# First two layers of a six-layer transformer pass: the norm at each seam by token tile instead of by column half

## The reference, cut to what matters

```
h = rms_norm(x, pre_mix_norm[l])
proj = h @ w_in[l]                       # 1024 x 2464
mix = concat(four attentions(proj))      # 256 x 1024
mix = mix @ w_o[l]
x = x + rms_norm(mix, post_mix_norm[l])
h = rms_norm(x, pre_ffn_norm[l])
gate, up = split(h @ ffn_w_gate_up[l])   # 1024 x 5632
f = (silu(gate) * up) @ ffn_w_down[l]    # 2816 x 1024
x = x + rms_norm(f, post_ffn_norm[l])
# rms_norm(x, w) = x * rsqrt(mean(x*x) + 1e-6) * w
```

## Time and profile before

| | |
|---|---|
| median of 3 runs | 1873.91 us (1871.16 to 1876.33) |
| profiled execution | 1872.82 us, span 1871.0 us |
| TensorE busy | 1823.4 us, 97% of the span |
| VectorE, ScalarE, GpSimd busy | 65%, 51%, 6% |
| mean granted TensorE clock | 0.996 of full speed |
| weights read | 309.90 MB, 167 GB/s over the span |

### The profile page before, as it was taken

How to read it: one execution, slowest core, us unless ns; L and a number is a source line. 1 busy time by engine, 2 the same in 40 slices (tenths; PEclk the granted TensorE clock), 3 DMA queues, 4 the chain that set the end, 5 groups by cost and what they waited for, 6 DMA issues and landing times.

```text
span 1871.0 us, 26055 instructions
## 1 busy us (share of the span) xinstructions
PE 1823.4 (97%) x9972; PEld 1533.6 (82%) x9972; DVE 1207.3 (65%) x1741; ACT 952.7 (51%) x1322; POOL 110.7 (6%) x152
## 2 busy tenths in 40 slices
PE   7999999999999999999999999999999999999999
PEld 6778888877888878788888788888778888878887
DVE  6576656867666588765565566557766556766555
ACT  5574444566544467644445554445254445665443
POOL 1400000150000030000000000003300001000000
PEclk9999999999999999999999999999999999999999
DMA  7604565641555656155554335554725554525552
GB/s 257 193 23 168 182 201 190 185 166 41 172 183 184 219 165 209 35 181 199 183 211 150 135 133 188 203 195 159 206 91 198 201 185 166 194 91 179 190 203 79
DMA packets 186216, 313.00 MB, mean 167 GB/s; under 512 B 17886, under 2 KB 69396, under 8 KB 186132
## 3 DMA queue, kind: packets, MB, share of 16 engines
q1 hardware_dynamic: 182883, 304.24, 48.3%
q0 software_dynamic: 1104, 3.50, 0.8%
q10 hardware_dynamic: 2144, 4.12, 0.7%
HBM read 309.90 MB, written 1.94 MB: 167 GB/s over the span
## 4 chain that ended last, share of the span: by engine, by line
PE 57%; DVE 4%; ACT 1%; issue 0%; POOL 0%; ACTq 0%; DVEq 0%
PE acc L2143 10%; PE acc L2144 10%; PE acc L2145 10%; PE up L2713 5%; PE tr L2713 5%; PE tr L2720 3%; PE up L2720 3%; PE acc L2713 2%; DVE tiles L1988 1%; PE acc L2720 1%; PE acc L2461 1%; PE up L2143 1%; PE up L2145 1%; PE up L2144 1%; PE tr L2321 1%; PE up L2422 1%
## 5 line engine op out<-in xcount | busy, mean ns | idle before, releaser
L1515 DVE TENSOR_TENSOR w_lo<-raw,w_hi 128x2048 fp32r<-128x2048 f32 (+2 forms) x290 | 654.5, 2288 | 177.1 <-ACT w_hi L1014 175.6
L1014 ACT ACTIVATE w_hi<-raw 128x2048 fp32r<-128x2048 f32 (+2 forms) x290 | 534.0, 1879 | 104.2 <-PE tr L2720 55.9
L2143 PE MATMUL acc<-w_hi,hT 128*128 128x512 f32 (+3 forms) x672 | 260.9, 388 | 3.2 <-DVE w_lo L1515 1.2
L2145 PE MATMUL acc<-w_hi,hT 128*128 128x512 f32 (+3 forms) x672 | 257.7, 383 | 0.0
L2144 PE MATMUL acc<-w_lo,hT 128*128 128x512 f32 (+3 forms) x672 | 257.4, 383 | 0.0
L2143 PE MATMUL acc<-w_hi,aux_hi 128*128 128x512 f32 x608 | 237.1, 390 | 0.0
L2144 PE MATMUL acc<-w_lo,aux_hi 128*128 128x512 f32 x608 | 237.1, 390 | 0.0
L2145 PE MATMUL acc<-w_hi,aux_lo 128*128 128x512 f32 x608 | 236.5, 389 | 0.0
L2713 PE MATMUL up<-hT,w_hi 128*128 128x512 f32 x768 | 191.6, 391 | 0.7 <-DVE w_lo L1515 0.7
L2713 PE MATMUL tr<-hT,w_hi 128*128 128x512 f32 x768 | 189.7, 389 | 0.0
L2713 PEld LDWEIGHTS tr<-hT,w_hi 128*128 128x128 f32 x768 | 144.2, 188 | 29.9
(11 more groups left out here) (386 smaller groups left out, 2249.6 us busy)
## 6 DMA issues: line engine op xcount, KB each, us to landing
raw<-in_mlp_w_up SPq DMA_DIRECT2D x64, 1024.0 KB, 6.5
raw<-in_mlp_w_down SPq DMA_DIRECT2D x64, 1024.0 KB, 5.4
raw<-in_ffn_w_gate_up SPq DMA_DIRECT2D x88, 512.0 KB, 4.7
raw<-in_ffn_w_down SPq DMA_DIRECT2D x22, 1024.0 KB, 5.0
raw<-in_w_in SPq DMA_DIRECT2D x16, 1024.0 KB, 8.7
raw<-in_sb_w_in SPq DMA_DIRECT2D x12, 1024.0 KB, 5.3
raw<-in_moba_w_in SPq DMA_DIRECT2D x12, 1024.0 KB, 5.4
raw<-in_w_o SPq DMA_DIRECT2D x8, 1024.0 KB, 6.2
```

Source lines behind the costliest of these rows:

```text
L1014: nc.scalar.activation(w_hi[:, p0.slot, 0:p0.floats], raw[:, p0.slot, 0:p0.floats], ACT.Copy)\
L1515: nc.vector.tensor_tensor(w_lo[:, p0.slot, 0:m], raw[:, p0.slot, 0:m], f32(w_hi[:, p0.slot, 0:m]), ALU.subtract).then_inc(sem["lo_ready"], 1)
L2143: nc.tensor.matmul(dst, hi, whi, start=first, stop=False)
L2145: return nc.tensor.matmul(dst, lo, whi, start=False, stop=last)
```

## The change

At the four seams everything goes by token tile.

- `closing` (w_o's last column half): token tile outside, pieces inside. `tile_done` follows tile 0's eight k, `piece_used` each piece's use by tile 1. Before the last two k of tile 1 TensorE transposes the first 512 columns of tile 0's new x (`turn_of`). The feed-forward's last step raises `tile_done` for each of its blocks.
- VectorE makes the root by tile (`y_root`), adds 512 columns of one tile at a time, and puts hT_lo of tile 0 between (`turned_lo_of`, 128 wide).
- The filler matmuls go; four transposes at a time (`turn_of`) stand between parts of the next matrix.
- `opening` (w_in and its like) does tile 0's high products, then its low ones, then tile 1. `first_hidden` (feed-forward, step 0) does three of the four hidden tiles for 128 tokens first, then for the other 128; the fourth hidden tile stays 256 wide.
- The plan: behind a feed-forward of these layers the turn of slots goes on with slot 3 (`align(3)`), so the next matrix's first piece has a slot that the feed-forward doesn't use; its split stands ahead of the last hidden step's sums on ScalarE and VectorE.

The core of the diff:

```diff
@@ class Plan
-    def align(self):
-        self.ring_start = len(self.pieces)
+    def align(self, slot=0):
+        self.ring_start = len(self.pieces) - slot
@@ make_plan, behind a feed-forward of layers 0 and 1
-            plan.align()
+            plan.align(3)
...
@@ ScalarE: gemm
                     if ph.out == "y":
                         act.wait_ge(sem["tile_done"], n["tile_done"] + i + 1)
                         y_square(sum_bank(ph, i, 0), 0, i)
+                        if i == len(ph.chunks) - 1:
+                            turned_hi(ph.then, 0, 0)
                         act.wait_ge(sem["piece_used"], pieces[-1][0] + 1)
                         y_square(sum_bank(ph, i, 1), 1, i)
...
@@ VectorE: gemm, last column half of w_o
+                            y_root(t)
+                            if t == 0:
+                                y_added(0, 0, W)
+                                y_gain(ph, sum_bank(ph, i, 0), 0, i)
+                                y_added(0, W, D)
+                                turned_lo_of(ph.then, 0, 0)
+                            else:
+                                y_added(1, 0, W)
+                                turned_lo_of(ph.then, 0, 1)
+                                y_gain(ph, sum_bank(ph, i, 1), 1, i)
+                                y_added(1, W, D)
...
@@ VectorE: feed-forward, behind the last step
+                    gain(0, 0)
+                    dve.wait_ge(sem["y_sq"], n["y_sq"] + 2)
+                    y_root(0)
+                    y_added(0, 0, W)
+                    gain(0, 1)
+                    y_added(0, W, D)
+                    dve.wait_ge(sem["y_sq"], n["y_sq"] + 4)
+                    y_root(1)
+                    gain(1, 0)
+                    y_added(1, 0, W)
+                    turned_lo_of(ph.then, 0, 0)
+                    turned_lo_of(ph.then, 0, 1)
+                    gain(1, 1)
+                    y_added(1, W, D)
...
@@ TensorE
+            def turn_of(base, t, half):
+                pe.wait_ge(sem["x_written"], base + 2 * t + half + 1)
+                for k in range(PK * half, PK * half + PK):
+                    last = nc.tensor.transpose(turned_tile(t, k), x[:, t, P * k:P * k + P], ident)
+                last.then_inc(sem["hT_tr"], 1)
...
+            def opening(ph):
...
+                one, two = pieces
+                pe.wait_ge(sem["lo_ready"], one[0] + 1)
+                high(0, *one)
+                turn_of(base, 0, 1)
+                pe.wait_ge(sem["lo_ready"], two[0] + 1)
+                high(0, *two)
+                turn_of(base, 1, 0)
+                low(0, *one)
+                low(0, *two)
+                turn_of(base, 1, 1)
+                for piece in pieces:
+                    high(1, *piece)
+                    low(1, *piece).then_inc(sem["piece_used"], 1)
...
+            def closing(ph, i, n0, w, pieces):
+                for t in range(TT):
+                    for p, k0, kt in pieces:
+                        slot = plan.pieces[p].slot
+                        if t == 0:
+                            pe.wait_ge(sem["lo_ready"], p + 1)
+                        whi, wlo = piece_view(w_hi, slot, 0, kt, w), piece_view(w_lo, slot, 0, kt, w)
+                        for k in range(kt):
+                            kk = k0 + k
+                            if (t, k0, k) == (1, PK, 2):
+                                turn_of(n["x_written"], 0, 0)
+                            last = three(sum_bank(ph, i, t), hT_hi[:, kk, P * t:P * t + P], hT_lo[:, kk, P * t:P * t + P],
+                                         whi[:, k, :], wlo[:, k, :], kk == 0, kk == KT - 1)
+                        if t == 1:
+                            last.then_inc(sem["piece_used"], 1)
+                    if t == 0:
+                        last.then_inc(sem["tile_done"], 1)
...
+            def first_hidden(ph):
...
+                early = (0, 1, 2)
+                pe.wait_ge(sem["lo_ready"], ph.first + 1)
+                high(0, 0, P, early)
+                low(0, 0, P, early)
+                pe.wait_ge(sem["lo_ready"], ph.first + 2)
+                high(1, 0, P, early)
+                turn_of(base, 1, 0)
+                low(1, 0, P, early)
+                high(0, P, S, early)
+                turn_of(base, 1, 1)
+                low(0, P, S, early)
+                high(0, 0, S, (3,))
+                low(0, 0, S, (3,)).then_inc(sem["piece_used"], 1)
+                high(1, P, S, early)
+                low(1, P, S, early)
+                high(1, 0, S, (3,))
+                low(1, 0, S, (3,)).then_inc(sem["piece_used"], 1)
```

More of the change, by code:

```diff
@@ L342, in make_plan @@
             a.then, b.before = b, ("y" if a.out == "y" or a.variant == "A" else "x")
+            if b.before == "y":
+                b.counts.update({"hT_tr": 2 * TT, "hT_hi": TT * KT, "hT_lo": TT * KT})
         if a.kind == "norm":
@@ L1427, in ffn @@
                     early = ph.variant == "B" and steps[0] == 0
+                    final = steps[0] == ph.n - 1
                     if early:
@@ L2226, in gemm @@
                             pe.wait_ge(sem["evac_d"], n["evac_d"] + i - 1)
+                    if ph.opens is not None and ph.opens.before == "y" and i == 0:
+                        opening(ph)
+                        continue
+                    if ph.out == "y" and i == len(ph.chunks) - 1:
+                        closing(ph, i, n0, w, pieces)
+                        continue
                     for p, k0, kt in pieces:
@@ L2656, in mix_conv, with weights @@
                 keep_clock(tr[:, 0, 0:S], 3)
[L2658 to L2660 removed]
+            def first_hidden(ph):
+                base, hi, lo = n["x_written"] - Y_WRITES, n["hT_hi"] - TT * KT, n["hT_lo"] - TT * KT
+                slots = [plan.pieces[ph.first + j].slot for j in range(ph.ups)]
+                def weights(buf, j, a, k):
                     at = PK * CH_A * (a // 2) + CH_A * k + P * (a % 2)
[L2662 to L2676 removed]
@@ new lines, in weights, with high @@
+                    return buf[:, slots[j], at:at + P]
+                def high(j, first, end, which):
+                    for k in range(PK):
+                        kk = PK * j + k
+                        pe.wait_ge(sem["hT_hi"], hi + KT * (end // P - 1) + kk + 1)
+                        for a in which:
+                            dst, src = first_sums[a][:, first:end], hT_hi[:, kk, first:end]
+                            nc.tensor.matmul(dst, weights(w_hi, j, a, k), src, start=kk == 0, stop=False)
+                            nc.tensor.matmul(dst, weights(w_lo, j, a, k), src, start=False, stop=False)
@@ new lines, in low @@
+                def low(j, first, end, which):
+                    for k in range(PK):
+                        kk = PK * j + k
+                        pe.wait_ge(sem["hT_lo"], lo + KT * (end // P - 1) + kk + 1)
+                        for a in which:
+                            last = nc.tensor.matmul(first_sums[a][:, first:end], weights(w_hi, j, a, k), hT_lo[:, kk, first:end],
+                                                    start=False, stop=kk == KT - 1)
+                    return last
@@ L2681, in hidden @@
                 def hidden(i, steps):
-                    for j in range(ph.ups):
+                    if ph.variant == "A" and steps[0] == 0:
+                        first_hidden(ph)
+                    for j in range(ph.ups if ph.variant == "B" or steps[0] > 0 else 0):
                         ps_ = [plan.pieces[ph.first + j if c == 0 else ph.first + ph.ups + ph.per * (c - 1) + j]
```

165 lines of the change are left out of this document (78 added, 87 removed).

## The result

| | before | after |
|---|---|---|
| median | 1874.82 us (4 runs, 1871.16 to 1876.33) | 1885.60 us (4 runs, 1883.98 to 1886.55) |
| ratio | | 1.0058, 95% interval 1.0046 to 1.0071 |
| profiled execution, span | 1872.82 us, 1871.0 us | 1885.99 us, 1884.1 us |

The changed kernel is 0.6% slower. Of its profile, first the page's busy times (the counterpart of the earlier trace rows): TensorE has 96 matmuls more (144 by the halved products, 48 fewer by the filler) and stays at 97%.

What follows compares the result with a forecast made beforehand. TensorE, busy 97% of the span, was taken as the bound, with gains only from its gaps. 3.55 + 8.75 + 1.5 - 0.5 - 2.2 + 0.3 = +11.4 us, giving 1885 us; range 1871 to 1893.

Steps and rivals of the forecast that it cites:

- Price of the narrow matmul: Feed-forward opening: a matmul of 128 columns behind a 128-column load costs 0.1115 us, between 0.060 and 0.125.
- The 0.060 row: Profile row with 30 weight columns loaded, 128 columns going every 0.06 us; taken as the lower bound of the price.
- First seam: w_o to feed-forward in layer 0: waits hidden, 20.6 us against 17.07, +3.55 us.
- Third seam: w_o to feed-forward in layer 1: +3.55 and a 5.2 us TensorE wait behind a late-freed slot, +8.75 us.
- Rival 2: No stall in layer 1: the slot is free in time or the wait passed otherwise; +4.7, 1878 us, chance 0.09.
- rival 1: Cheap loads: an fp32r load of 128 weight columns hides under 128 streamed columns; -3.6, 1870 us, chance 0.14.
- Clock behind it: Behind layer 1's stall after w_o: the idle stretch may lower TensorE's clock; 1.5 us put in, between 0 and 3.4.
- Second seam: Feed-forward to next input matrix in layer 0: early end paid back as a wait for w_lo, -0.5 us.
- Fourth seam: Feed-forward to next input matrix in layer 1: one VectorE split now ahead of its gains, -2.2 us (0 to -2.8).
- Layer 2's output matrix: Left one slot off by the ring; its feed-forward's second piece split some 5 us later, +0.3 us.
- The sum: Whole kernel: the terms add to +11.4 us on 1872.8, carried over to 1885 us, 0.6% slower.
- Rival 3: Clock falls in the opening, narrow matmuls at 0.213 us; +18 to +30, 1895 us, chance 0.07.

Runs made afterwards that it cites:

- e2: Changed kernel with two hidden tiles instead of three made for the first 128 tokens alone; 1882.02 us, 1.0047 of the kernel before.
- e3: Changed kernel, early part of the first feed-forward step streaming only 64 of 128 tokens per tile behind the same weight loads; 1916.95 us, one run.
- e4: Changed kernel with the split of the feed-forward's second piece behind tile 0's square and turn; 1878.24 us, 1.0021 of the kernel before.
- e1: Changed kernel with the turn of slots begun anew with slot 0 before w_o; 1881.38 us, 1.0042 of the kernel before.
- e12: Changed kernel with 11 filler matmuls of 256 columns in layer 1 ahead of the transposes TensorE waits for; 1884.63 us, one run.
- e13: Kernel before with only the shifted turn of slots and the early split of the next matrix's first piece; 1873.12 us, 0.9991 of the kernel before.
- e10: Changed kernel with layer 1's feed-forward in slots 3, 0 and 1 instead of 0, 1 and 2; 1884.84 us, 1.0055 of the kernel before.
- e6: Changed kernel without the shifted turn of slots and the early split; 1881.68 us, 1.0037 of the kernel before.
- e8: Changed kernel with w_o and the first feed-forward step as in the kernel before; 1871.22 us, 0.9985 of the kernel before.
- e5: Changed kernel with 40 filler matmuls of 256 columns in layer 1 ahead of the transposes TensorE waits for; 1894.83 us, one run.

## Why the prediction was right

- **Price of the narrow matmul, 0.1115 us.** Measured 0.11, and 2.50 us a tile (e2). It came from the row with one streamed column, and e3 shows why that row was the right one: behind this load 1, 64 and 128 streamed columns cost the same. The 0.060 row had another load.
- **First seam, all waits hidden, +3.55.** Measured +3.63.
- **Third seam, the wait.** Place, chain and size held: 5.05 us for 5.2, and each link stands in the trace at the forecast distance. e4 takes it away by the place of the split, e1 by the slot. Rival 2 is refuted by the wait itself, rival 1 by the price.
- **Clock behind it, 1.5 taken between 0 and 3.4.** 1.76 by e12. That a clock loss comes was argued from the earlier trace rows, but 1.5 was picked and not worked out, so that it lies this near is luck; behind the same stall in e2 the loss was 0.3 less. The whole seam is 10.64 for 10.25: 3.63 + 5.05 + 1.76 = 10.44. Most of the missing 0.2 is how a wait is counted: the 5.05 begin at the end of a record of 0.39 us, and by starts, as everything else here, it is 478.40 - 472.96 - 0.23 = 5.21.
- **Second seam, -0.5.** -0.32: the early end came and was paid back as a wait for w_lo, 0.82 us, as said.
- **Fourth seam, -2.2.** -2.43. The reason given, that one split is now ahead, is half of it: alone it gives -0.97 (e13), with the order by tile the rest.
- **Layer 2's output matrix, +0.3.** 0.00 there. I had taken a split 5 us later as a cost; nothing waited for it.
- **The sum.** The four seams and layer 2 add 11.48 us where +11.4 was forecast. The terms are off by +0.1, +0.2, +0.4, -0.2 and -0.3, so that the sum is nearer than its terms is luck too.
- **The first stretch, +1.59,** is in no term and belongs to this one execution: the profiled executions differ by 13.2 us, the medians by 10.8.

Rival 3, the clock that falls in the opening, stayed away in the changed kernel and came in e3 at its price of 0.213 a matmul. Its size was too small: it put 3.3 us at a seam for one stretch of half clock of 6.6 us, and in e3's first seam half clock lasted 30.7 us. Why the clock held with 128 streamed columns and not with 64 is not shown.

One figure of rival 1 does not follow from the rest: at 2.9 us for each 0.01 the +11.4 are used up at a price of 0.072, not at 0.077. The measured 0.11 is far from both.

## What to carry to other kernels

Halving the streamed side of a matmul saves nearly nothing per matmul where the weight load alone takes as long as the whole matmul did (here 0.111 us against 0.118), and it doubles their number. Price it by the row with the fewest columns behind the same load, and keep it wide if the wait that it would fill is shorter than what it adds.

A split or copy that waits for a buffer holds up all that stands behind it in its engine's queue. When slots or the order of freeing change, list for each such instruction which use frees its slot and what stands behind it, at every seam that the rotation reaches: three choices of slots here (changed, e1, e10) had the stall at three places, and e4 lost it by moving the split and no slot.

Two edits at one seam may not add up. Here one lost alone (e6, +1.9 and +1.3), the other gave little alone (e13, 0.0 and -1.0), and together they gained (e8, -0.3 and -2.4). So undo each of them before you price them.

## What the runs showed of the hardware that was not expected

- In e3 TensorE, with 64 streamed columns behind 128-column loads, lost its full clock after 5 us though it was busy without a gap (granted clock 0.50 from 151.3 to 182.0 us); in the changed kernel, with 128 columns in the same step, the granted clock stayed 1.00.
- The weight load follows the granted clock: in e3, with 64 streamed columns matmuls start 0.11 apart at 1.00 and 0.21 apart at 0.50.
- One filler matmul of 256 columns with plain float32 operands takes 0.43 us (e5: 80 records, two to a filler, in 17.43 us), nearly four times an fp32r product of 256 columns at 0.118.
